# A two-layer transformer block on one core: x also read in turned, token roots applied in PSUM, the convolution shared among three engines, position biases laid out beforehand

## The reference

```python
hn = rms_norm(h, mix_pre_g)              # x * rsqrt(mean(x*x) + eps) * g, per token
proj = hn @ w_in                         # 1024 x 1792: q 512, k 128, v 128, u 1024
attn_out = sliding_window_attention(q, k, v, attn_sinks, rel_bias)
# conformer_conv(u):
a, gate = jnp.split(u, 2, axis=-1)
h = a * jax.nn.sigmoid(gate)             # 1024 tokens x 512 channels
h = depthwise_conv(h, conv_dw, width=31, causal) + conv_dw_b
h = silu(layer_norm(h, conv_ln_g, conv_ln_b)) @ w_conv_pw
```

## Time and profile before

| | before |
|---|---|
| median of 3 runs | 2305.56 us (2305.15 to 2306.09) |
| the profiled execution | 2305.78 us |
| its span | 2304.0 us |
| PE busy | 2279.3 us (99%) |
| DVE busy | 1399.7 us (61%) |
| ACT busy | 973.3 us (42%) |
| POOL busy | 918.8 us (40%) |
| mean granted clock | 0.999 |

### The profile page before, as it was taken

The page is one execution under the profiler, slowest core; times in us unless marked ns, Lnnn a source line. Parts: engine busy times, 40 slices in busy tenths (PEclk is TensorE's granted clock), DMA queues, the critical chain, the costliest instruction groups (busy, mean ns, idle before and its releaser), DMA issues.

```text
span 2304.0 us, 30846 instructions
## 1 busy us (share of the span) xinstructions
PE 2279.3 (99%) x11604; PEld 1904.6 (83%) x11604; DVE 1399.7 (61%) x2229; ACT 973.3 (42%) x1980; POOL 918.8 (40%) x813
## 2 busy tenths in 40 slices
PE   9999899999999999999999999999999999999998
PEld 8787688888888888888898878888888888888887
DVE  7999715945444477776533676154594444447776
ACT  4126734433232344455634765135443323234543
POOL 2014535488787700033112032221448878770003
PEclk9999999999999999999999999999999999999999
DMA  5222134233233368665002001243223323336865
GB/s 160 53 64 79 51 102 146 65 119 119 87 120 105 126 241 289 209 217 136 19 11 71 24 10 37 69 169 110 101 68 107 124 86 126 104 120 247 294 213 191
DMA packets 219590, 275.85 MB, mean 120 GB/s; under 512 B 17260, under 2 KB 144973, under 8 KB 216627
## 3 DMA queue, kind: packets, MB, share of 16 engines
q1 hardware_dynamic: 200594, 210.31, 29.3%
q10 hardware_dynamic: 18848, 63.58, 7.0%
HBM read 205.27 MB, written 68.57 MB: 119 GB/s over the span
## 4 chain that ended last, share of the span: by engine, by line
PE 92%; DVE 3%; ACT 2%; issue 1%; POOL 1%; DMA 0%; POOLq 0%; DVEq 0%; ACTq 0%
PE P L497 27%; PE P L499 27%; PE P L498 27%; PE P L3159 3%; PE P L3178 2%; PE P L3194 2%; PE P L509 1%; PE P L3116 1%; DVE acc L1235 1%; PE P L793 0%; DVE s L1725 0%; ACT p L3257 0%; DVE stats L3327 0%; PE P L1522 0%; POOL stats L572 0%
## 5 line engine op out<-in xcount | busy, mean ns | idle before, releaser
L497 PE MATMUL P<-ah,wh 128*128 128x512 f32 (+1 forms) x1136 | 441.4, 389 | 0.6 <-ACT go L2503 0.5
L499 PE MATMUL P<-ah,wl 128*128 128x512 f32 (+1 forms) x1136 | 438.9, 386 | 0.0
L498 PE MATMUL P<-al,wh 128*128 128x512 f32 (+1 forms) x1136 | 438.7, 386 | 0.0
L497 PE MATMUL P<-wh,ah 128*128 128x512 f32 (+2 forms) x1128 | 426.0, 378 | 0.0
L499 PE MATMUL P<-wh,al 128*128 128x512 f32 (+2 forms) x1128 | 423.4, 375 | 0.0
L498 PE MATMUL P<-wl,ah 128*128 128x512 f32 (+2 forms) x1128 | 423.0, 375 | 0.0
L579 POOL TENSOR_TENSOR stats<-stats,epsc 128x1 f32<-128x1 f32 x78 | 32.0, 411 | 647.6 <-ACT xn L2005 421.0
L497 PEld LDWEIGHTS P<-ah,wh 128*128 128x128 f32 x1136 | 213.5, 188 | 43.7 <-ACT go L2503 0.8
L499 PEld LDWEIGHTS P<-ah,wl 128*128 128x128 f32 x1136 | 213.4, 188 | 43.1
L498 PEld LDWEIGHTS P<-al,wh 128*128 128x128 f32 x1136 | 213.5, 188 | 42.2
L499 PEld LDWEIGHTS P<-wh,al 128*128 128x128 f32 x1128 | 212.2, 188 | 37.2
(11 more groups left out here) (384 smaller groups left out, 4377.4 us busy)
## 6 DMA issues: line engine op xcount, KB each, us to landing
rf<-ff_rows SPq DMA_DIRECT2D x154, 256.0 KB, 5.2
stage<-in_w_down_dram SPq DMA_DIRECT2D x110, 256.0 KB, 3.8
ff_rows<-sb ACTq DMA_DIRECT2D x22, 1024.0 KB, 5.0
stage<-in_w_gu_dram SPq DMA_DIRECT2D x44, 512.0 KB, 5.1
stage<-in_w_in_dram SPq DMA_DIRECT2D x22, 512.0 KB, 4.0
stage<-in_w_gate_dram SPq DMA_DIRECT2D x22, 512.0 KB, 4.1
stage<-in_w_up_dram SPq DMA_DIRECT2D x22, 512.0 KB, 5.1
ff_rows<-uo ACTq DMA_DIRECT2D x22, 512.0 KB, 3.0
```

The lines of the kernel that those rows point to most:

```text
L497: e.matmul(out, lh, rh, start=start, stop=False, skip_group_check=onto)
L498: e.matmul(out, lh, rl, start=False, stop=False, skip_group_check=onto)
L499: return e.matmul(out, ll, rh, start=False, stop=stop, skip_group_check=onto)
```

## The change

The host now hands in further arrays. `x_turned` is x transposed, `x_gains` the gain by channel, `conv_taps` the 31 taps, bias, gain and offset by channel, and `near_bias` and `far_bias` the two bias tables, which ACT only negates after they have landed. The making of tables on the chip, their stores and the skewed loads go.

Since x comes turned, no row is normalised and turned at the start: ACT multiplies the turned x by the gain into `AH`, DVE makes `AL`, and PE forms its products without the roots of the tokens. x is read in a second time as rows only for ACT's sums of squares. One root per token is spread over 128 partitions by PE (`token_roots_pe`) and kept in `roots` (128x1024). DVE multiplies each finished PSUM bank by it: gates into `SG`, from which ACT takes the sigmoid, and values, k, v and q in place in the bank (`rooted`).

The convolution is divided. Channel chunk 0 is done by ACT, which multiplies `hp` by a tap into one of two buffers (`tap_products`), and POOL, which adds it to `acc`. Chunk 2 is shared: DVE does taps 0 to 15 over 1024 columns ("whole"), ACT and POOL the others. Chunks 1 and 3 stay with DVE, in even and odd halves, with their sums in PSUM banks 2 and 3. No tap is left for the next stage.

```diff
-    lows_by_dve = {*range(1, 22), *range(first["chunk"], first["chunk"] + 4)}
+    lows_by_dve = {*range(22), *range(first["chunk"], first["chunk"] + 4)}
...
-    SPLIT = (1, 2, 3)
+    SPLIT = (1, 3)
+    tap_products = [sb(f"tap_product{i}", [128, 1024], off["extra"] + 256 + 4 * KB * i) for i in range(2)]
+    roots = sb("token_roots", [128, 1024], off["extra"] + 256 + 8 * KB)
...
+        load_to(3)
+        e.dma_start(cwt[:, :, :], I["conv_taps"]).then_inc(*l_misc.up("taps"))
+        e.dma_start(sinks[:, :], I["attn_sinks"].partition_broadcast(128)).then_inc(*l_misc.up("all"))
+        for t in range(8):
             row(t)
...
+    def x_root(th):
+        DV.wait_ge(sq, ("x", 4 * th + 3))
+        DV.e.tensor_scalar(col(72 + 4 * th, 4), col(64 + 4 * th, 4), EPS, None, ALU.add).then_inc(*sm.up(("x", th)))
...
+    SHARED = 16
+    def add_taps(c):
         if c in SPLIT:
+            taps.extend(in_turn([("even", c, j) for j in range(16)], [("odd", c, j) for j in range(1, 16)]) + [
+                (name, c, 0) for name in ("rows", "edge", "first", "both")] + [("sum", c, j) for j in range(16)] + [("out", c, 0)])
         else:
+            taps.extend(("whole", c, w) for w in range(SHARED))
...
+    PRODUCTS = [(0, a, a + 512, w) for a in (0, 512) for w in range(TAPS)]
+    PRODUCTS += [(2, 0, 1024, w) for w in range(SHARED, TAPS)]
+    def some_products(n):
+        e = AC.e
+        while products and n > 0:
+            c, a, b, w = products.pop(0)
...
+                if k >= 2:
+                    c2, a2, _, w2 = ADDED[k - 2]
+                    AC.wait_ge(pt, (c2, a2, w2))
+                e.activation(tap_products[k % 2][:, 0:b - a], src, ACT.Copy, scale=weight).then_inc(*ep.up((c, a, w)))
+            n -= (b - a) / 512
+    def pool_taps(c):
...
+                PL.e.tensor_tensor(acc[:, c, a:b], acc[:, c, a:b], tap_products[k % 2][:, 0:b - a], ALU.add).then_inc(
+                    *pt.up((c, a, w)))
...
+        for t in range(8):
+            x_square(t)
         gate(0, 0)
+        gate(1, 0)
+        products.extend(PRODUCTS)
+        some_products(6)
+        gate(1, 1)
         send_to(4)
+        some_products(8)
...
+        for i, name in enumerate(KVQ):
+            for th in range(2):
+                kv_copy(name, th)
+                if th == 0:
+                    send_to(c + i + 3)
+                some_products(4)
...
+        x_root(0)
+        x_root(1)
+        token_roots_dve(0)
+        gate(0, 0)
+        values(0, 0)
         glu(0, 0)
...
         for c in range(2, 4):
             for th in range(2):
+                gate(c, th)
+                low_by_dve_to(2 * c + 2 + th)
+                some_taps(5)
+                values(c, th)
+                glu(c, th)
+                some_taps(5)
+            add_taps(c)
+        for i, name in enumerate(KVQ):
+            for th in range(2):
+                rooted(KVQ_BANKS[name][th], th, (name, th), mm, (name, 0, th))
                 some_taps(6)
+                if th == 0:
+                    low_by_dve_to(first["kvq"] + i + 3)
...
-        PL.wait_ge(pz, "kp1")
+        PL.wait_ge(pt, (2, 0, TAPS - 1))
         for i in range(2):
             sink_column(i)
```

More of the change, by code:

```diff
@@ L1032, in skewed_load @@
[L1032 to L1037 removed]
+            if t >= 5:
+                SP.wait_ge(sq, ("x", t - 5))
+            e.dma_start(x0[t % 5][:, :], I["x"][128 * t:128 * t + 128, :]).then_inc(*l_x0[t % 5].up(t))
+        turned(0, 1, 0)
+        turned(1, 1, 0)
@@ new lines, in input_loads @@
+        for k in range(2, 8, 2):
+            turned(k, 2, 0)
+        loaded[0] = 1
+        load_to(1)
+        SP.wait_ge(ah, ("x", 3, 0))
+        turned(0, 4, 1)
+        load_to(2)
+        SP.wait_ge(ah, ("x", 7, 0))
+        turned(4, 4, 1)
+        load_to(3)
+        e.dma_start(cwt[:, :, :], I["conv_taps"]).then_inc(*l_misc.up("taps"))
+        e.dma_start(sinks[:, :], I["attn_sinks"].partition_broadcast(128)).then_inc(*l_misc.up("all"))
+        for t in range(8):
+            row(t)
@@ L1148, in mixer1_pe @@
+        u_unit(1, 0, 1)
+        token_roots_pe(1)
+        u_unit(1, 1, 1)
+        for i in range(2):
+            u_unit(0, i, 1)
         PE.ends("u0")
@@ L1179, in in_turn @@
         return mixed
-    def split_ops(c):
-        return in_turn([("even", c, j) for j in range(16)], [("odd", c, j) for j in range(1, 16)]) + [
-            (name, c, 0) for name in ("both", "rows", "first")] + [("sum", c, j) for j in range(16)]
+    SHARED = 16
     def add_taps(c):
         if c in SPLIT:
-            taps[:] = in_turn(taps, split_ops(c))
-        else:
-            taps[:] = in_turn(taps, [(c, w, 512, 1024) for w in range(FIRST_HALVES)] + [
-                (c, w, 0, 1024) for w in range(FIRST_HALVES, TAPS)])
@@ L1208, in split_op @@
             DV.wait_ge(zf, "hp")
-        if name == "even":
+            if c > 1:
+                DV.wait_ge(tap, ("out", 1, 0) if c == 2 else ("whole", 2, SHARED - 1))
+        if name == "whole":
+            both = PF[:, 512 * TAP_BANKS[0]:512 * TAP_BANKS[0] + 1024]
+            if j == 0:
+                ins = e.tensor_scalar(both, hp[:, c, 0:1024], cwt[:, c, 0:1], bias, ALU.mult, ALU.add)
+            else:
+                behind("whole")
+                ins = e.scalar_tensor_tensor(acc[:, c, :] if j == SHARED - 1 else both, hp[:, c, j:j + 1024],
+                                             cwt[:, c, j:j + 1], both, ALU.mult, ALU.add)
+        elif name == "even":
@@ L1284, in mixer1_act @@
-        x_square(3)
+            AC.wait_ge(ev, ("gate", c, th))
+            e.activation(SG[th][:, :], SG[th][:, :], ACT.Sigmoid).then_inc(*gl.up(("u", c, th)))
+        first_loads(AC)
+        first_piece_hi(0)
+        for k in range(4):
+            x_turned_hi(k, 0)
+        first_piece_hi(1)
+        for k in range(4, 8):
+            x_turned_hi(k, 0)
+        sent[0] = 1
         send_to(1)
-        hi(2)
-        hi(3)
-        x_square(4)
-        x_square(5)
+        for k in range(4):
+            x_turned_hi(k, 1)
@@ L1401, in mixer1_dve @@
+        token_roots_dve(0)
+        gate(0, 0)
+        values(0, 0)
+        glu(0, 0)
+        gate(1, 0)
+        values(1, 0)
+        glu(1, 0)
+        token_roots_dve(1)
+        gate(1, 1)
+        low_by_dve_to(4)
+        values(1, 1)
+        glu(1, 1)
+        add_taps(1)
+        some_taps(4)
+        gate(0, 1)
+        some_taps(6)
+        values(0, 1)
         glu(0, 1)
         low_by_dve_to(5)
-        add_taps(0)
-        some_taps(14)
-        glu(1, 1)
-        low_by_dve_to(6)
@@ L1511, in swa_pe @@
         e = PE.e
+        for b in TAP_BANKS:
+            held[b] = (tap, ("out", SPLIT[-1], 0))
         def scores(i):
@@ L1562, in conv_turn @@
             for c in range(4):
-                PE.wait_ge(tap, ("sum", c, 15) if c in SPLIT else (c, TAPS - 1))
+                PE.wait_ge(*((tap, ("out", c, 0)) if c in SPLIT else (pt, (2, 0, TAPS - 1))))
             for c in range(4):
@@ L3470, in chunk_in_act @@
         send_to(c + 8)
+        AC.wait_ge(l_b2, "all")
+        e.activation(b2[:, :, :], b2[:, :, :], ACT.Copy, scale=-1.0).then_inc(*nb.up("b2"))
         for t in range(CV_EARLY):
@@ L4440, in sync_program @@
             stored(SP, name)
-        for i in range(3):
-            SP.wait_ge(l_sk[i], "all")
         SP.wait_ge(l_kv, "all")
```

520 lines of the change are left out of this document (232 added, 288 removed).

## The result

The changed kernel takes 2317.93 us, the median of 4 runs (2316.59 to 2318.21), against 2305.65 before. The ratio is 1.0053, with a 95% interval of 1.0039 to 1.0068: slower, by 12.3 us. The prediction had 2311, with a range of 2299 to 2322. Its profiled execution has a span of 2314.8 us, 10.8 more than before; it is the fastest of the four (2316.59), so 1.5 of the 12.3 us stand in no trace.

A forecast was written before the change was run, and what follows sets the result against it. PE bounded the kernel before; DVE's chain would set the attention's start: 40 + 123.9 + 21.6 = 185.5, plus 4.5 gives 190.0, +8.6. With -4.9 and +1.7 in the attention, +5.4 gives 2311 us, range 2299 to 2322.

The forecast's parts named there:

- What bounds afterwards: First stage, up to the attention: DVE's chain with its waits ends at 185.5 us, after PE's last unit near 171.
- Start of DVE's chain, 40: After x's rows, their squares and seven DVE operations, the chain starts at 40 us; bounds 37.5 and 43.5.
- Work, 123.9: DVE's taps, multiplications and low parts from its chain's start to q3's last multiplication take 123.9 us.
- rival 5: DVE's taps of chunks 1 and 3: PSUM as destination is dearer, 0.065 us each, giving 2319; chance 0.08.
- Waits and locks, 21.6: DVE's waits before q3's end: chunk 4 5.6, chunk 5 1.3, four steps 8.7, low parts against POOL's adds 6.0 us.
- To the first exponential, 4.5: Behind q3: ACT's copy 0.6, last product 1.05, POOL's add 2.37, sink columns and hand-overs 0.5; together 4.5 us.
- Sum to the mark, +8.6: The mark, the window attention's first exponential, comes at 190.0 us against 181.40 before: 8.6 later.
- The attention gives back 4.9: Window attention: the 3.32 us wait for a low part and 1.6 of slow clock behind it go, -4.9 us.
- The clock at its beginning costs 1.7: Beginning of the attention: PE idles from 171 to 190 and pays the slow clock behind it once, +1.7 us.
- POOL's adds, 1.36 apart: First stage: POOL's adds on its own result are spaced 1.36 us and keep it busy over 120 us by 190.
- PE's own end, 171: First stage: PE finishes its last unit near 171 us, then waits 15 us or more at the attention's beginning.
- The tables, nothing: Bias tables from outside: their making goes, ACT's negations of b1 and b2 lie under other time; worth nothing.

The follow-up runs named there:

- experiment 2: Changed kernel with DVE's low parts of chunks 6 to 9 placed behind the five taps that follow them; 2312.40 us.
- Experiment 3: Changed kernel with eight of the fifteen wide products of chunk 2 left out (taps 16 to 23 not computed); 2309.67 us.
- experiment 6: Changed kernel with DVE's sums of chunks 1 and 3 in SBUF instead of PSUM banks 2 and 3; 2374.17 us.
- Experiment 4: Kernel before, with the taps left over for the attention not computed, but for the last of each chunk of channels; 2299.94 us.
- experiment 1: Changed kernel with chunk 4's weight copy and the second gate's sigmoid behind two tap products instead of six; 2317.44 us.
- experiment 7: Changed kernel, same instructions reordered on ACT and DVE: experiments 1 and 2 joined, narrow products through before q0, the table's negation later; 2311.81 us.

## Why the prediction was right, and where it was off

The sign and the mechanism were right, and 2317.93 lies in the range. The size was half: +5.4 forecast, +12.3 measured. By its own steps:

- **What bounds afterwards.** Right: DVE's chain, not PE and not POOL's amount of work (experiments 2 and 3).
- **Start of DVE's chain, 40.** Its low part of chunk 4 was due at 42.5, where the prediction had 41.2: 1.3 late. Of that 0.3 came from the squares (the first multiplication at 36.28, forecast 35 to 36). The seven operations and their hand-overs took 5.6 us (35.49 to 41.05) instead of 4.8.
- **Work, 123.9.** Right. From the start, 41.3, to the end of q3's multiplication, 191.3, are 150.0; without waits and locks (below, 25.8) 124.2. The SBUF price for a destination in PSUM was right (experiment 6), so the forecast's rival 5 is out.
- **Waits and locks, 21.6.** This term was mis-sized: 25.8. The prediction's items hold a lock beside the wait, so the low part's time over 1.22 us is counted with each. Chunk 4: 5.13 + 0.48 = 5.6 (5.6). Chunk 5 with its sigmoid: 1.1 (1.3). Four steps: 7.3 + 1.0 = 8.3 (8.7; by its own parts, 2.25 each, it should have read 9.0). The seven low parts of k, v and q: 5.3 (6.0). So every item that it named was right or slightly dear, 1.3 us in all. Two things it had at nothing made up the difference, 5.5 us. One is the lock of the two additions of even and odd rows, both of whose operands lie in SBUF: 2.8. The other is the wait at q1, 2.7: the copy stood behind wide products, the copies of v and the negation of b1 (1.91), which I had put under POOL's adds at no cost.
- **To the first exponential, 4.5.** Measured 4.5, in the order forecast.
- **Sum to the mark, +8.6.** Measured +14.4: 1.3 from the start, 4.2 from waits and locks, 0.3 from work. So of the 6.9 us between 5.4 and 12.3, 5.8 lie ahead of the mark, 0.4 were won more behind it, and 1.5 are the profiled execution's distance from the median.
- **The attention gives back 4.9.** Experiment 4 gives 5.2. **The clock at its beginning costs 1.7.** The changed kernel's rest is 1.6 longer than experiment 4's (2119.0 against 2117.4), but that is not the clock's price by itself: PE also waits 6.2 us for POOL there instead of 3.4, and a rest is known to about 1 us. The mean granted clock was 0.68 from 180 to 200; how much of the 1.6 is due to it no run separates, and the match in size may be luck. Net 3.6 against 3.2.
- **POOL's adds, 1.36 apart.** They were 1.44 apart in the first stage. Experiment 3 shows that POOL's total does not set the mark; what 0.08 per add costs through ACT's list ahead of a copy was not tested.
- **PE's own end, 171.** Wrong without consequence: 182.6. It began its first unit at 12.26, since the unit matrix landed only at 7.2 and 24 transposes of it came first; the waits were 12.3 us instead of 9.4; and it had a slow stretch (below). So it waited 12.0 us at the attention (8.3 and 3.7) and not 15 or more.
- **The tables, nothing.** Inside this change, where PE waits anyway, no loss by it shows; but on the kernel before they are worth 3.7 us, the only part shown to win by itself.

What the sum can't show is that the waits don't add up. Taking away the largest gave nothing (experiment 1), four others 5.1 of 7.3 (experiment 2), and all of them by reordering no more than 4.3 at the mark (experiment 7). In experiment 1 PE's units came up behind the wait that went; in experiment 7 ACT's list tied the copies for DVE to POOL's adds. What is settled is the account of the whole: the change takes 25 us of DVE's work out of the attention, where it cost 5.2, and in return the attention starts 14.4 us later.

Not settled is how the loss divides between the turned x and the division of the convolution; no run has one without the other. The turned x is a rival for all of it: 24 of its multiplications by roots stand in DVE's chain from 41.3 us on, by an estimate 24 x 0.61 = 14.6 us, and the kernel before has none of them. Not tried is a kernel that keeps the leftover taps on DVE in the attention together with the division; chunk 3's sums would have to leave banks 2 and 3 for it.

## What to carry to other kernels

Work of an engine that is not on the path should be moved only after measuring what it costs where it is: 25 us of taps cost 5.2 in the attention, and there the same number of columns costs some two and a half to three times as much on ACT and POOL. When work is shared through an engine that also feeds the path, count the operations that stand ahead of each feeding copy, not the total of the helper. And try the parts of a change alone: here one part won 3.7 us, the others hid it, and two of them were never told apart.

## What was not expected of the hardware

Behind the wait of 8.77 us for v, PE's matmuls of 512 columns took 0.63 us instead of 0.39 from the first unit on until 149.4:

```profile
143.81 1.94 PE L1154 MATMUL P<-ident,v1t 128*128 128x128 f32 x8 [8.77 <-ACT v1t L1349]
...
145.97 0.63 PE L513 MATMUL P<-al,wh 128*128 128x512 f32 x1
```

The stretches, in the order of the others:

```profile
140.00:145.00 5.00, 1.19 (x6) 1.22 (x7) 5.00 (x7) 2.51 (x4) 3.98 (x3) 0.50 0.23 68
145.00:150.00 5.00, 5.00 (x16) 4.04 (x15) 5.00 (x9) 3.62 (x5) 4.49 (x4) 0.54 0.12 37
150.00:155.00 5.00, 5.00 (x24) 4.13 (x23) 5.00 (x8) 1.93 (x3) 4.74 (x5) 1.00 0.19 57
```

A granted clock of 0.50 is the level of 1.2 GHz, and it was there after one idle time; from 145 to 150 PE got through 16 matmuls and in the next 5 us through 24, 8 x 0.23 = 1.8 us. This wait cost PE its own length and then about that. The kernel's time doesn't show it, as PE waited again at the attention.
